# The modulation of the second block moved behind the projections of the first mixer, and four PSUM banks for projections

## The chip, the cores and the metric

The kernel runs on one core of one Trainium2 chip. The metric is the device time of one execution in microseconds (us). A measurement of this kernel is the median of several executions.

## The reference, cut to what matters

The reference is a transformer of two blocks on 256 tokens of width 1024, in float32. The first block is a hybrid mixer and a mixture of experts. The second is another mixer and another mixture, whose normed inputs are scaled and shifted by a modulation. The modulation depends on two small vectors alone and so can be computed at any time before the second block:

```
def modulation(cvec, w_ada, b_ada):          # w_ada: 1024 x 6144
    m = jax.nn.silu(cvec) @ w_ada + b_ada
    return jnp.split(m, 6, axis=-1)

def hybrid_mixer(n, w_in, gla_gate_w2, gla_gate_b, gla_norm_g, w_out):
    proj = n @ w_in                           # 1024 x 3088
    gq, gk, gv, gr, glr, aq, ak, av = jnp.split(proj, IN_SPLITS, axis=-1)
    log_a = jax.nn.log_sigmoid(glr @ gla_gate_w2 + gla_gate_b) / GLA_TAU
    o_gla = norm(gla_chunked(gq, gk, gv, log_a)) * jax.nn.silu(gr)
    o_att = three dilated softmax attentions of aq, ak, av
    return concatenate([o_gla, o_att]) @ w_out
```

## The kernel before

`mixer1` computes the first mixer and, between its steps, the modulation. Each engine has one list of instructions in a fixed order; semaphores tie the lists together.

**Weights.** All large weights come in pieces of 2 MB (1024 rows by 512 columns) into a ring of six slots, `weight_ring`. SyncE (SP) issues the loads one after the other, and for each it first waits until the slot's last reader is done. In `mixer1` these are the six pieces of `w_in` (0 to 5), the twelve pieces of `w_ada_2` for the modulation (ADA+0 to ADA+11), the two of `w_out` (WO, WO+1), and then four pieces of the first experts' weights for the phase that follows. `read_order` is the order in which the pieces are read, so that a load takes the slot that comes free first: w_ada pieces 0 to 5 are read between the projections, and their slots are free again for later pieces.

**Projections.** `project(j)` is one of 21 jobs on TensorE (PE). It multiplies the normed input `nT` by a part of a w_in piece (8 matmuls of 256 or 512 columns) into PSUM bank 4 + j % 2, and `take(j)` on ScalarE (ACT) copies the bank out. Job j waits until job j - 2 has been copied. `ps` has eight banks.

**The rest of PE's list.** `scores` and `p_transposes` belong to the attention, `weighted_values` is its last product. `level(l)` for l from 0 to 8 is a step of the gated linear attention. VectorE (DVE) makes its operand `M` (lines 708, 709) from `Dl` (line 684) after ACT has put `Dl` through an exponential (lines 523, 524), and copies the result out under a mask (line 694). The matmuls of line 443 give the output of the gated attention, DVE norms it, and `merge` (line 449) multiplies the result by `w_out` in two halves: the first (k from 4 to 7) needs the attention alone, the second the normed output.

**Modulation.** `mod_piece(i)` (line 390) multiplies 32 columns of `mcs` by w_ada piece i into bank 7, four matmuls side by side on column strips. `take_mod(i)` on ACT copies the bank out, and `mod_total(i)` (line 374) sums the strips into bank 6. PE's list has one such piece behind this or that projection or level: piece 0 behind project(10), 1 behind project(15), 2 behind the P transposes, 3 to 6 between levels and projections 17 to 20, 7 to 11 behind `weighted_values`. Projections 18 and 20 are cut in halves (`early`, `late`) around a level. After the modulation's last sum come line 443 and the merges.

```
            for half in range(2):
                pe.wait_ge(*has_come(WO + half))
            pe.wait_ge(s_pvtk, 2)
            merge(0, 0, range(4, 8))
```

PE waits here for both pieces of `w_out` before the first merge.

**After the mixer** `moe` begins behind a barrier of all engines: router, then a loop over the experts whose weights come through the same ring.

Of the kernel before, what the change touches and what calls it, by code (L numbers as in the profile page):

```python
# [12 lines left out]
P = 128  # L13
# [3 lines left out]
KD = D // P  # L17
# [111 lines left out]
def mixer1(c, t, mod):  # L129

    nc, ps, h = c.nc, c.ps, c.h
    with phase(nc, "m1_") as (st, sb, sem):
# [71 lines left out]
        w_cols = [1552, 2064, 0, 1024, 512, 2576]  # L204
        jobs = [("T", 0, i) for i in range(4)] + [("T", 1, i) for i in range(4)] + [("T", 2, i) for i in range(4)] + \
# [6 lines left out]
        ADA, WO, NX = 6, 6 + NP_, 8 + NP_  # L212
        read_order = [0, 1, ADA, 2, ADA + 1, 3, ADA + 2, ADA + 3, 4, ADA + 4, ADA + 5, 5] + [ADA + i for i in range(6, NP_)]
        label = {}
        slots = list(range(6))
        for x in range(6, NX):
            slots.append(slots[read_order[x - 6]])
        for s_, x in zip((3, 4, 0, 1, 2, 5), [WO, WO + 1] + read_order[NX - 6:]):
            label[slots[x]] = s_
        slots = [label[s_] for s_ in slots]  # L220
        nth = [slots[:x].count(slots[x]) + 1 for x in range(NX)]

        def has_come(x):
            return s_w[slots[x]], 16 * nth[x]

        def read(x):
            return (s_proj, done_with[x]) if x < 6 else (s_mpart, x - ADA + 1)
# [3 lines left out]
        @block.sync  # L231
        def _(sp):
            xv = t["x"].rearrange("b (t p) d -> p (b t) d", p=P)
            for tt in range(TT):
                sp.dma_start(h[:, tt, :], xv[:, tt, :]).then_inc(s_x[tt], 16)

            def load(x, w, a):
                if x >= 6:
                    sp.wait_ge(*read(read_order[x - 6]))
                sp.dma_start(piece(c, slots[x]), w[0, :, a:a + 512].rearrange("(k p) n -> p k n", p=P)).then_inc(s_w[slots[x]], 16)  # L240

            for x, a in enumerate(w_cols):
                load(x, t["w_in"], a)
            for i in range(NP_):
                load(ADA + i, t["w_ada_2"], i * BANK)
            for i in range(2):
                load(WO + i, t["w_out"], i * 512)
            W = [t[x] for x in ("expert_w1", "expert_w3", "expert_w2")]
            for x in read_order[NX - 6:]:
                sp.wait_ge(*read(x))  # L250
                load_one(c, sp, c.s_e1, slots[x] // 3, slots[x] % 3, W)
# [24 lines left out]
        @block.tensor  # L276
        def _(pe):
# [8 lines left out]
            def project(j, ks=range(KD)):  # L286
                kind, x, i = jobs[j]
                bank = 4 + j % 2
                if j >= 2 and ks[0] == 0:
                    pe.wait_ge(s_evac, j - 1)  # L290
                if kind in "TN" and i == 0:
                    pe.wait_ge(*has_come(x))
                w = piece(c, slots[x]) if kind in "TN" else None
# [3 lines left out]
                else:  # L297
                    if kind == "lr":
                        pe.wait_ge(s_lrw, 48)
                    for k in ks:  # L300
# [9 lines left out]
                if kind == "z" or ks[-1] == KD - 1:  # L310
                    last.then_inc(s_proj, 1)
# [21 lines left out]
            def weighted_values():  # L333
                pe.wait_ge(s_PTe, len(PT_GROUPS))
                pe.wait_ge(s_evac, NJ)
                for hh in range(4):
                    for it in range(TT):
                        for jt in range(it + 1):
                            for par in range(2):
# [3 lines left out]
                                last = pe.matmul(ps[par * 64:par * 64 + 64, 4 + hh // 2, at:at + P], av[:, jt, a * AHD:(a + 1) * AHD], p,  # L343
# [34 lines left out]
            def mod_piece(i):  # L378
                pe.wait_ge(*has_come(ADA + i))
                if i == 0:  # L380
                    pe.wait_ge(s_mcs, 1)
                    pe.wait_ge(s_pick, 1)
                    pe.wait_ge(s_mb, 16)
                    pe.matmul(ps[:, 6, 0:2 * NC], brow[:], each[:].rearrange("p k r -> p (k r)"), start=True, stop=False, skip_group_check=True)
                if i >= 1:
                    pe.wait_ge(s_mptk, i)
                w = piece(c, slots[ADA + i])
                for k in range(KD):
                    j = k % 4
                    last = pe.matmul(ps[32 * j:32 * j + 32, 7, :], mcs[:, k, :], w[:, k, :], start=(k < 4), stop=(k >= 4))  # L390
# [4 lines left out]
            early, late = range(0, 4), range(4, KD)  # L395
# [20 lines left out]
            project(18, early)  # L416
            level(1)
            project(18, late)
            mod_piece(4)
            level(2)  # L420
            project(19)
            level(3)
            mod_piece(5)
            project(20, early)
            level(4)
            project(20, late)
            mod_piece(6)
            level(5)
            weighted_values()
            mod_piece(7)  # L430
            level(6)
            mod_piece(8)
            mod_piece(9)
            level(7)
            mod_piece(10)
            mod_piece(11)
            level(8)
            mod_total(NP_ - 1)
            pe.wait_ge(s_Atk, NLV + 1)
            for i2 in range(TT):  # L440
# [4 lines left out]
                last.then_inc(s_og, 1)  # L445

            def merge(tt, half, ks):
                for k in ks:
                    last = pe.matmul(ps[:, 4 + 2 * half + tt, :], nT[:, k, tt * P:(tt + 1) * P], piece(c, slots[WO + half])[:, k, :],
# [23 lines left out]
        def _(act):  # L473
# [17 lines left out]
            def take(j):  # L491
                kind, x, i = jobs[j]
                bank = 4 + j % 2
# [19 lines left out]
            def take_mod(i):  # L513
# [3 lines left out]
                act.activation(mpart[:, i % 2, :], ps[:, 7, :], ACT.Copy).then_inc(s_mptk, 1)  # L517
# [8 lines left out]
            act.wait_ge(s_mc, 32)  # L526
            act.wait_ge(s_mz, 1)
            act.activation(mcs[:, :, 0:2], mc[:], ACT.Silu).then_inc(s_mcs, 1)
# [4 lines left out]
            take_mod(0)  # L533
            take(11)
            exps(1)
            for j in range(12, 16):
                take(j)
            take_mod(1)
# [9 lines left out]
            take_mod(2)  # L548
            take(17)
            level(1)  # L550
            take_mod(3)
            level(2)
            take(18)
            take_mod(4)
            level(3)
            take(19)
            level(4)
            take_mod(5)
            level(5)
            take(20)  # L560
            take_mod(6)
            level(6)
            for b in range(2):
                act.wait_ge(s_pv, b + 1)
                act.activation(catA[:, 2 * b:2 * b + 2, :].rearrange("p k n -> p (k n)"), ps[:, 4 + b, :], ACT.Copy).then_inc(s_pvtk, 1)
            take_mod(7)
            level(7)
            take_mod(8)
            take_mod(9)
            level(8)  # L570
            take_mod(10)
            take_mod(11)
# [1882 lines left out]
```

## Time and profile before

| | us |
|---|---|
| median of 3 runs | 1833.49 |
| lowest, highest | 1826.11, 1833.73 |
| the profiled execution: its own time | 1827.63 |
| the profiled execution: span from first to last instruction | 1825.5 |

Times within the span are counted from its first instruction. The profile tells for each engine when its instructions ran, what released them when they waited, what the DMA engines moved, and which clock TensorE was granted (1.00 is full speed, 0.50 the lower level). A line of the timeline has start, duration, engine, line of the code, operation, output and inputs, and the count of instructions merged into it. The records count two matmuls for each one of the code.

### The profile page before, as it was taken

How to read it: one execution, taken by the hardware profiler on the slowest of the kernel's cores; microseconds unless marked ns; L12 is line 12 of the kernel's file. 1: busy time of each engine (PE TensorE's matmuls, PEld its weight loads, DVE VectorE, ACT ScalarE, POOL GpSimd, SP SyncE). 2: the span in 40 equal slices, each digit the busy share in tenths (PEclk: the TensorE clock that was granted, in tenths of full speed). 3: DMA queues.
4: the chain of work that ended last, by engine and by line, in shares of the span. 5: the costliest groups of instructions: out<-in, count | busy, mean ns of one | idle time of the engine just before them, and what ended most of it. 6: DMA issues, size and time to landing. Idle time of an engine off the chain costs nothing. (4 is left out here: it accounts for less than half of the span.)

```text
span 1825.5 us, 29532 instructions
## 1 busy us (share of the span) xinstructions
PE 1465.0 (80%) x12551; PEld 975.3 (53%) x12551; DVE 628.8 (34%) x1703; ACT 258.1 (14%) x546; POOL 42.4 (2%) x61
## 2 busy tenths in 40 slices
PE   7999578999878887489998998989376666666664
PEld 6555345666555565279766746876243343333332
DVE  3533445222122332404765633432341222222224
ACT  2421221111011111021100212230010000000000
POOL 1000000000000000010000100000000000000000
PEclk9999689999888999789999999989688888888887
DMA  9677659999999999593231242244449999999994
GB/s 344 241 258 290 176 226 415 411 414 412 411 410 410 408 414 420 195 291 115 73 136 69 104 150 92 96 147 178 148 174 422 422 423 422 423 422 420 422 421 201
DMA packets 155736, 530.55 MB, mean 291 GB/s; under 512 B 38312, under 2 KB 56816, under 8 KB 139264
## 3 DMA queue, kind: packets, MB, share of 16 engines
q1 hardware_dynamic: 152016, 525.40, 73.1%
q0 software_dynamic: 1200, 3.77, 0.6%
q8 instruction: 68, 1.11, 0.2%
q10 hardware_dynamic: 2432, 0.10, 0.1%
q14 instruction: 20, 0.16, 0.0%
HBM read 528.19 MB, written 1.06 MB: 290 GB/s over the span
## 5 line engine op out<-in xcount | busy, mean ns | idle before, releaser
L1341 PE MATMUL ps<-weight_ring,e_xT 128*32 128x256 f32 x4096 | 310.1, 469 | 197.6 <-DMA weight_ring<-in_w_up_dram 134.7
L1341 PEld LDWEIGHTS ps<-weight_ring,e_xT 128*32 128x32 f32 x4096 | 173.8, 134 | 330.2 <-issue 284.2
L1363 PE MATMUL ps<-weight_ring,e_gT 128*32 128x256 f32 x2048 | 124.9, 385 | 17.7 <-DVE e_gT L1566 17.7
L1564 DVE TENSOR_TENSOR e_g<-e_act_g,ps 128x128 f32<-128x128 f32 x64 | 18.4, 287 | 300.2 <-ACT e_act_g L1407 299.1
L1363 PEld LDWEIGHTS ps<-weight_ring,e_gT 128*32 128x32 f32 x2048 | 60.3, 110 | 68.4 <-DVE e_gT L1566 28.8
L1563 DVE TENSOR_TENSOR e_act_g<-e_act_g,ps 128x128 f32<-128x128 f32 x32 | 9.2, 288 | 224.1 <-ACT e_act_g L1407 224.0
L1407 ACT ACTIVATE e_act_g<-ps 128x128 f32<-128x128 f32 x64 | 17.7, 277 | 478.1 <-PE ps L1341 478.1
L1318 PE MATMUL ps<-e_y,e_GwT 32*128 32x256 f32 x1056 | 75.6, 400 | 1.2 <-DVE e_GwT L1581 1.2
L961 PE MATMUL ps<-e_nT,e_ctx_w 128*128 128x256 f32 x320 | 72.3, 385 | 4.1 <-DVE e_ctx_gcols L1061 3.4
L1305 PE MATMUL ps<-e_n,e_Gt 128*32 128x256 f32 x1056 | 70.1, 381 | 0.0
L961 PEld LDWEIGHTS ps<-e_nT,e_ctx_w 128*128 128x128 f32 x320 | 61.0, 193 | 12.7 <-issue 3.6
L1566 DVE COPY e_gT<-ps 128x128 f32<-128x128 f32 x64 | 18.6, 291 | 133.9 <-PE ps L1311 133.9
L1318 PEld LDWEIGHTS ps<-e_y,e_GwT 32*128 32x128 f32 x1056 | 47.8, 184 | 29.8 <-issue 26.3
L1890 PEld LDWEIGHTS ps<-m_Q,weight_ring 128*128 128x128 f32 x480 | 56.2, 192 | 9.4 <-DVE m_Q L2191 5.7
L1890 PE MATMUL ps<-m_Q,weight_ring 128*128 128x128 f32 x480 | 57.3, 276 | 4.7 <-DVE m_Q L2191 4.7
L963 PE MATMUL ps<-e_ctx_w,e_nT 128*128 128x256 f32 x256 | 58.7, 382 | 0.5 <-DVE e_ctx_kw L1067 0.5
L1950 PE MATMUL ps<-weight_ring,m_nTp 128*128 128x512 f32 x128 | 58.4, 617 | 0.0
L1994 PE MATMUL ps<-m_nT,weight_ring 128*128 128x256 f32 x256 | 56.8, 382 | 0.0
L1855 PE MATMUL ps<-m_nT,weight_ring 128*128 128x256 f32 x256 | 56.4, 379 | 0.0
L1866 PE MATMUL ps<-weight_ring,m_nT 128*128 128x512 f32 x128 | 56.3, 592 | 0.0
L1994 PEld LDWEIGHTS ps<-m_nT,weight_ring 128*128 128x128 f32 x256 | 49.2, 192 | 6.9
L963 PEld LDWEIGHTS ps<-e_ctx_w,e_nT 128*128 128x128 f32 x256 | 47.4, 190 | 9.0 <-issue 2.3
(485 smaller groups left out, 1936.7 us busy)
## 6 DMA issues: line engine op xcount, KB each, us to landing
weight_ring<-in_expert_w_dram SPq DMA_DIRECT2D x96, 2048.0 KB, 20.4
weight_ring<-in_w_down_dram SPq DMA_DIRECT2D x32, 2048.0 KB, 24.6
weight_ring<-in_w_gate_dram SPq DMA_DIRECT2D x32, 2048.0 KB, 19.2
weight_ring<-in_w_up_dram SPq DMA_DIRECT2D x32, 2048.0 KB, 23.7
weight_ring<-in_w_in_dram SPq DMA_DIRECT2D x26, 2048.0 KB, 8.4
weight_ring<-in_w_ada_dram SPq DMA_DIRECT2D x12, 2048.0 KB, 7.9
e_ctx_w<-in_w_in_dram SPq DMA_DIRECT2D x18, 1024.0 KB, 22.2
weight_ring<-in_w_out_dram SPq DMA_DIRECT2D x4, 2048.0 KB, 10.3
```

The lines of the kernel that those rows point to most:

```text
L961: mm = pe.matmul(o, w[:, k, j * P:(j + 1) * P], nT[:, k, :], start=(k == 0), stop=(k == KD - 1))
L963: mm = pe.matmul(o, nT[:, k, j * P:(j + 1) * P], w[:, k, :], start=(k == 0), stop=False)
L1305: mm = pe.matmul(ps[32 * j:32 * j + 32, 5, 0:256], Gt[:, tt, :], n[:, tt, j * 256:(j + 1) * 256], start=(tt == 0), stop=(tt == TT - 1))
L1318: mm = pe.matmul(ps[:, m, tt * 256:(tt + 1) * 256], GwT[r, tt * P:(tt + 1) * P], y[r, :], start=False, stop=False, skip_group_check=True)
L1341: mm = pe.matmul(ps[32 * j:32 * j + 32, 4, 0:256].rearrange("p (w f) -> p w f", w=2), xT[:, k % 2, k // 2, :], w13[:, :, k, j * P:(j + 1) ...
L1363: mm = pe.matmul(ps[32 * m:32 * m + 32, 5, 0:256], gT[:, j * 32:(j + 1) * 32], w2[:, j, m * 256:(m + 1) * 256], start=(j == 0), stop=(j == ...
L1566: dve.tensor_copy(gT[:], ps[:, 4, 0:P]).then_inc(s_gT, 1)
L1855: mm = pe.matmul(ps[:, 4 + j % 4, 0:T], w[:, k, (j % 4) * P:(j % 4 + 1) * P], nT[:, k, :], start=(k == 0), stop=(k == KD - 1))
L1866: mm = pe.matmul(ps[:, 4 + j % 4, :], nT[:, k, tile * P:(tile + 1) * P], w[:, k, :], start=(k == 0), stop=(k == KD - 1))
L1890: mm = pe.matmul(o, a, b, start=True, stop=True)
L1950: mm = pe.matmul(ps[:, j % 4, :], nTp[:, k, tile * P:(tile + 1) * P], w[:, k, :], start=(k == 0), stop=(k == KD - 1))
L1994: mm = pe.matmul(ps[:, 2 + f % 2, 0:T], w[:, k, j * P:(j + 1) * P], rhs[:, k, :], start=(k == 0), stop=(k == KD - 1))
```

## The change

All twelve pieces of the modulation are moved behind `weighted_values` and level 4. The projections come first and use four banks (4 + j % 4), and job j waits for job j - 4. The modulation has banks 4 and 5 in turn for its products and 6 for its sums. `weighted_values` goes to banks 6 and 7. Pieces 0 and 1 stand before level 5, then two behind each of levels 5 and 6, two behind level 7, piece 8 behind level 8, and 9 to 11 behind the matmuls of line 443. Projections 18 and 20 are whole. The slots of the ring are taken in turn: w_ada piece i waits for the last projection that reads w_in piece i (i below 6), piece i from 6 on for `mod_piece(i - 6)`, the two pieces of w_out for `mod_piece(6)` and `mod_piece(7)`, the experts' four for pieces 8 to 11. Two small loads of `mod_c` by GpSimd (POOL) come later in its list, and the Silu that reads them moves behind take(12).

```diff
         w_cols = [1552, 2064, 0, 1024, 512, 2576]
+        RING = [3, 4, 0, 1, 2, 5]
...
             for x, a in enumerate(w_cols):
                 load(x, t["w_in"], a)
             for i in range(NP_):
-                load(ADA + i, t["w_ada_2"], i * BANK)
+                if i < 6:
+                    sp.wait_ge(s_proj, done_with[i])
+                else:
+                    sp.wait_ge(s_mpart, i - 5)
+                load(6 + i, t["w_ada_2"], i * BANK)
             for i in range(2):
+                sp.wait_ge(s_mpart, NP_ - 5 + i)
                 load(WO + i, t["w_out"], i * 512)
...
-            pool.dma_start(mc[:, :, 0], t["c_2"].rearrange("o (k p) -> p (o k)", p=P), allow_slow_non_contiguous=True).then_inc(s_mc, 16)
-            pool.dma_start(mc[:, :, 1], t["c_ctx_2"].rearrange("(k p) -> p k", p=P), allow_slow_non_contiguous=True).then_inc(s_mc, 16)
...
+            pool.dma_start(mc[:, :, 0], t["c_2"].rearrange("o (k p) -> p (o k)", p=P), allow_slow_non_contiguous=True).then_inc(s_mc, 16)
+            pool.dma_start(mc[:, :, 1], t["c_ctx_2"].rearrange("(k p) -> p k", p=P), allow_slow_non_contiguous=True).then_inc(s_mc, 16)
             pool.dma_start(brow[:], t["b_ada_2"].rearrange("o (k p) -> (o k) p", p=P)).then_inc(s_mb, 16)
...
-            def project(j, ks=range(KD)):
+            def project(j):
                 kind, x, i = jobs[j]
-                bank = 4 + j % 2
-                if j >= 2 and ks[0] == 0:
-                    pe.wait_ge(s_evac, j - 1)
+                bank = 4 + j % 4
+                if j >= 4:
+                    pe.wait_ge(s_evac, j - 3)
...
             def mod_piece(i):
-                pe.wait_ge(*has_come(ADA + i))
+                pe.wait_ge(*has_come(6 + i))
                 if i == 0:
...
+                    pe.wait_ge(s_pvtk, 2)
...
-                if i >= 1:
-                    pe.wait_ge(s_mptk, i)
+                if i >= 2:
+                    pe.wait_ge(s_mptk, i - 1)
...
-            project(10)
-            mod_piece(0)
-            for j in range(11, 16):
+            for j in range(10, 17):
                 project(j)
-            mod_piece(1)
-            project(16)
             for g in range(len(PT_GROUPS)):
                 p_transposes(g)
-            mod_piece(2)
             project(17)
             level(0)
+            project(18)
+            level(1)
+            project(19)
+            level(2)
+            project(20)
+            level(3)
+            weighted_values()
+            level(4)
+            mod_piece(0)
+            mod_piece(1)
+            level(5)
+            mod_piece(2)
             mod_piece(3)
...
             pe.wait_ge(s_Atk, NLV + 1)
...
                 last.then_inc(s_og, 1)
+            for i in range(9, NP_):
+                mod_piece(i)
+            mod_total(NP_ - 1)
...
             for half in range(2):
                 pe.wait_ge(*has_come(WO + half))
-            pe.wait_ge(s_pvtk, 2)
+            merge(1, 1, range(4, 8))
+            pe.wait_ge(s_mptk, NP_)
             merge(0, 0, range(4, 8))
             merge(1, 0, range(4, 8))
-            merge(1, 1, range(4, 8))
```

On ACT the copies follow the same order: levels 1 to 4 with takes 18 to 20, the two copies of the attention's output, then for each of levels 5 to 8 its exponentials and two `take_mod`, then the last four.

## Rows read from the trace of the kernel before

**Rows 1.** The first line of the page.

```profile
span 1825.5 us, 29532 instructions
```

**Rows 2.** Stretches: busy us of each engine (instructions), granted clock, DMA share, GB/s.

```profile
56.00:112.00 56.00, 55.94 (x286) 28.24 (x286) 22.13 (x25) 21.92 (x34) 0.00 (x0) 1.00 0.67 239
112.00:156.00 44.00, 44.00 (x350) 24.34 (x346) 15.67 (x31) 9.61 (x21) 0.00 (x0) 1.00 0.90 337
156.00:160.40 4.40, 4.40 (x26) 4.40 (x26) 2.09 (x4) 0.28 (x2) 0.00 (x0) 0.61 0.95 394
160.40:189.60 29.20, 28.96 (x76) 12.97 (x74) 8.36 (x13) 1.22 (x3) 1.67 (x1) 1.00 0.32 127
189.60:248.00 58.40, 36.39 (x236) 23.73 (x236) 25.84 (x91) 14.97 (x28) 3.22 (x10) 0.71 0.53 144
248.00:740.00 492.00, 418.65 (x4686) 277.60 (x4682) 148.12 (x489) 74.73 (x179) 0.00 (x0) 0.92 1.02 411
```

**Rows 3.** PE's waits from 0 to 200 us: total, times, longest.

```profile
PE ps L283 <- ACT m_n L483: 10.2, 1, 10.2
PE ps L305 <- DMA weight_ring<-in_w_in_dram: 0.8, 1, 0.8
```

**Rows 4.** Timeline of PE from 0 to 190 us.

```profile
120.33 1.92 PE L390 MATMUL ps<-weight_ring,m_mod_silu 128*32 128x512 f32 x16
122.18 1.05 PE L374 MATMUL ps<-m_mod_pick,m_mod_part 128*128 128x2 f32 x8
123.09 3.68 PE L307 MATMUL ps<-weight_ring,m_nT 128*128 128x512 f32 x8
126.70 1.16 PE L368 MATMUL ps<-m_M 64*128 64x128 f32 x16
...
131.43 1.92 PE L390 MATMUL ps<-weight_ring,m_mod_silu 128*32 128x512 f32 x16
...
135.36 0.66 PE L343 MATMUL ps<-m_PT,m_av 128*64 128x128 f32 x8
...
138.13 1.92 PE L390 MATMUL ps<-weight_ring,m_mod_silu 128*32 128x512 f32 x16
...
156.07 4.57 PE L443 MATMUL ps<-m_gv,m_AT 128*128 128x128 f32 x24
160.48 13.90 PE L449 MATMUL ps<-weight_ring,m_nT 128*128 128x512 f32 x32
...
175.50 14.00 PE L449 MATMUL ps<-weight_ring,m_nT 128*128 128x512 f32 x32
```

**Rows 5.** Timeline of DVE and ACT from 110 to 160 us.

```profile
120.44 1.36 DVE L694 COPY_PREDICATED m_AT<-mask_f,ps 128x512 f32<-128x512 uint8 x2 [5.58 <-PE ps L368]
...
122.63 0.42 DVE L709 TENSOR_TENSOR m_M<-m_Dl,m_qT 128x256 f32<-128x256 f32 x1
...
138.24 0.60 ACT L565 ACTIVATE m_nT<-ps 128x512 f32<-128x512 f32 x1 [0.71 <-PE ps L343]
```

**Rows 6.** Timeline of SP's queue from 0 to 250 us.

```profile
28.42 103.47 SPq L240 DMA_DIRECT2D weight_ring<-in_w_ada_dram  x12
133.41 7.07 SPq L240 DMA_DIRECT2D weight_ring<-in_w_out_dram  x2
```

**Rows 7.** Issues on the page (KB, median us to landing), and a stretch with the queue full.

```profile
weight_ring<-in_w_ada_dram SPq DMA_DIRECT2D x12, 2048.0 KB, 7.9
...
40.00:44.00 4.00, 4.00 (x21) 3.51 (x20) 0.00 (x0) 0.38 (x1) 0.00 (x0) 1.00 1.05 386
```

**Rows 8.** Two stretches of 1 us at the start.

```profile
7.00:8.00 1.00, 0.00 (x0) 0.00 (x0) 0.08 (x1) 0.89 (x2) 0.00 (x0) 1.00 1.58 141
...
12.00:13.00 1.00, 1.00 (x6) 1.00 (x5) 0.72 (x2) 0.25 (x1) 0.92 (x1) 1.00 1.10 372
```

**Rows 9.** Three stretches of 1 us behind the mixer.

```profile
194.00:195.00 1.00, 0.00 (x0) 0.00 (x0) 0.37 (x3) 0.00 (x0) 0.51 (x1) 0.50 0.87 133
...
204.00:205.00 1.00, 0.64 (x3) 0.64 (x4) 0.30 (x1) 0.65 (x2) 0.19 (x1) 0.50 1.05 348
...
207.00:208.00 1.00, 0.90 (x5) 0.63 (x3) 0.00 (x0) 0.66 (x2) 0.00 (x0) 0.68 1.15 492
```

More of the change, by code:

```diff
@@ L210, in mixer1, with slot_of @@
         done_with = [max(j + 1 for j, job in enumerate(jobs) if job[1] == x) for x in range(6)]
[L212 to L221, printed above, removed]
+        def slot_of(x):
+            return RING[x % 6]
         def has_come(x):
-            return s_w[slots[x]], 16 * nth[x]
-        def read(x):
-            return (s_proj, done_with[x]) if x < 6 else (s_mpart, x - ADA + 1)
+            return s_w[slot_of(x)], 16 * (x // 6) + 16
+        WO = 6 + NP_
         block = st.enter_context(nc.Block())
@@ L237, in load @@
             def load(x, w, a):
-                if x >= 6:
-                    sp.wait_ge(*read(read_order[x - 6]))
-                sp.dma_start(piece(c, slots[x]), w[0, :, a:a + 512].rearrange("(k p) n -> p k n", p=P)).then_inc(s_w[slots[x]], 16)
+                sp.dma_start(piece(c, slot_of(x)), w[0, :, a:a + 512].rearrange("(k p) n -> p k n", p=P)).then_inc(s_w[slot_of(x)], 16)
             for x, a in enumerate(w_cols):
@@ L244, in _ @@
             for i in range(NP_):
-                load(ADA + i, t["w_ada_2"], i * BANK)
+                if i < 6:
[3 more added lines that the diff above has]
+                load(6 + i, t["w_ada_2"], i * BANK)
             for i in range(2):
+                sp.wait_ge(s_mpart, NP_ - 5 + i)
                 load(WO + i, t["w_out"], i * 512)
             W = [t[x] for x in ("expert_w1", "expert_w3", "expert_w2")]
-            for x in read_order[NX - 6:]:
-                sp.wait_ge(*read(x))
-                load_one(c, sp, c.s_e1, slots[x] // 3, slots[x] % 3, W)
+            for i, (u, which) in enumerate(((0, 0), (0, 1), (0, 2), (1, 2))):
+                sp.wait_ge(s_mpart, NP_ - 3 + i)
+                load_one(c, sp, c.s_e1, u, which, W)
         @block.gpsimd
@@ L284, in _ @@
                 last.then_inc(s_tr, 1)
-            def project(j, ks=range(KD)):
+            def project(j):
                 kind, x, i = jobs[j]
-                bank = 4 + j % 2
-                if j >= 2 and ks[0] == 0:
-                    pe.wait_ge(s_evac, j - 1)
+                bank = 4 + j % 4
+                if j >= 4:
+                    pe.wait_ge(s_evac, j - 3)
                 if kind in "TN" and i == 0:
                     pe.wait_ge(*has_come(x))
-                w = piece(c, slots[x]) if kind in "TN" else None
+                w = piece(c, slot_of(x)) if kind in "TN" else None
                 if kind == "z":
@@ L299, in project @@
                         pe.wait_ge(s_lrw, 48)
-                    for k in ks:
+                    for k in range(KD):
                         if j == 0 and k % 2 == 0:
@@ L309, in project @@
                             last = pe.matmul(ps[0:GLR, bank, 0:T], w_lr[:, k, :], nT[:, k, :], start=first, stop=end)
-                if kind == "z" or ks[-1] == KD - 1:
-                    last.then_inc(s_proj, 1)
+                last.then_inc(s_proj, 1)
             def scores(it, heads, bank):
@@ L342, in weighted_values @@
                                 at = (hh % 2) * T + it * P
-                                last = pe.matmul(ps[par * 64:par * 64 + 64, 4 + hh // 2, at:at + P], av[:, jt, a * AHD:(a + 1) * AHD], p,
+                                last = pe.matmul(ps[par * 64:par * 64 + 64, 6 + hh // 2, at:at + P], av[:, jt, a * AHD:(a + 1) * AHD], p,
                                                  start=(jt == 0), stop=(jt == it))
@@ L383, in mod_piece @@
                     pe.wait_ge(s_mb, 16)
+                    pe.wait_ge(s_pvtk, 2)
                     pe.matmul(ps[:, 6, 0:2 * NC], brow[:], each[:].rearrange("p k r -> p (k r)"), start=True, stop=False, skip_group_check=True)
-                if i >= 1:
-                    pe.wait_ge(s_mptk, i)
-                w = piece(c, slots[ADA + i])
+                if i >= 2:
+                    pe.wait_ge(s_mptk, i - 1)
+                w = piece(c, slot_of(6 + i))
                 for k in range(KD):
                     j = k % 4
-                    last = pe.matmul(ps[32 * j:32 * j + 32, 7, :], mcs[:, k, :], w[:, k, :], start=(k < 4), stop=(k >= 4))
+                    last = pe.matmul(ps[32 * j:32 * j + 32, 4 + i % 2, :], mcs[:, k, :], w[:, k, :], start=(k < 4), stop=(k >= 4))
                 last.then_inc(s_mpart, 1)
@@ L393, in mod_piece @@
                     mod_total(i - 1)
-            early, late = range(0, 4), range(4, KD)
             for j in range(9):
@@ L403, in _ @@
             scores(1, range(4, 8), 0)
-            project(10)
-            mod_piece(0)
-            for j in range(11, 16):
+            for j in range(10, 17):
                 project(j)
-            mod_piece(1)
-            project(16)
             for g in range(len(PT_GROUPS)):
                 p_transposes(g)
-            mod_piece(2)
             project(17)
             level(0)
+            project(18)
[10 more added lines that the diff above has]
+            mod_piece(2)
             mod_piece(3)
-            project(18, early)
-            level(1)
-            project(18, late)
+            level(6)
             mod_piece(4)
-            level(2)
-            project(19)
-            level(3)
             mod_piece(5)
-            project(20, early)
-            level(4)
-            project(20, late)
+            level(7)
             mod_piece(6)
-            level(5)
-            weighted_values()
             mod_piece(7)
-            level(6)
+            level(8)
             mod_piece(8)
[L433 to L438, printed above, removed]
             pe.wait_ge(s_Atk, NLV + 1)
@@ L445, in _ @@
                 last.then_inc(s_og, 1)
+            for i in range(9, NP_):
+                mod_piece(i)
+            mod_total(NP_ - 1)
             def merge(tt, half, ks):
                 for k in ks:
-                    last = pe.matmul(ps[:, 4 + 2 * half + tt, :], nT[:, k, tt * P:(tt + 1) * P], piece(c, slots[WO + half])[:, k, :],
+                    last = pe.matmul(ps[:, 4 + 2 * half + tt, :], nT[:, k, tt * P:(tt + 1) * P], piece(c, slot_of(WO + half))[:, k, :],
                                      start=(k == 4), stop=(k == 3))
@@ L492, in take @@
                 kind, x, i = jobs[j]
-                bank = 4 + j % 2
+                bank = 4 + j % 4
                 act.wait_ge(s_proj, j + 1)
@@ L516, in take_mod @@
                     act.wait_ge(s_msum, i - 1)
-                act.activation(mpart[:, i % 2, :], ps[:, 7, :], ACT.Copy).then_inc(s_mptk, 1)
+                act.activation(mpart[:, i % 2, :], ps[:, 4 + i % 2, :], ACT.Copy).then_inc(s_mptk, 1)
             def level(l):
@@ L524, in level @@
                 act.activation(d[:, :, 1, :], d[:, :, 1, :], ACT.Exp, scale=1.0 / 16).then_inc(s_E, 1)
-            act.wait_ge(s_mc, 32)
-            act.wait_ge(s_mz, 1)
-            act.activation(mcs[:, :, 0:2], mc[:], ACT.Silu).then_inc(s_mcs, 1)
             for j in range(10):
@@ L532, in _ @@
             take(10)
-            take_mod(0)
             take(11)
             exps(1)
-            for j in range(12, 16):
+            take(12)
+            act.wait_ge(s_mc, 32)
+            act.wait_ge(s_mz, 1)
+            act.activation(mcs[:, :, 0:2], mc[:], ACT.Silu).then_inc(s_mcs, 1)
+            for j in range(13, 16):
                 take(j)
-            take_mod(1)
             act.wait_ge(s_az, 1)
@@ L547, in _ @@
                 act.activation(dst, ps[:, g % 4, :].rearrange("p (a n) -> p a n", a=4), ACT.Copy).then_inc(s_PTe, 1)
-            take_mod(2)
             take(17)
[L550 to L556, printed above, removed]
-            level(4)
[L558 to L562, printed above, removed]
+            for l in range(1, 4):
+                level(l)
+                take(17 + l)
+            level(4)
             for b in range(2):
                 act.wait_ge(s_pv, b + 1)
[L565 to L572, printed above, removed]
+                act.activation(catA[:, 2 * b:2 * b + 2, :].rearrange("p k n -> p (k n)"), ps[:, 6 + b, :], ACT.Copy).then_inc(s_pvtk, 1)
+            for l in range(5, NLV + 1):
+                level(l)
+                take_mod(2 * (l - 5))
+                take_mod(2 * (l - 5) + 1)
+            for i in range(8, NP_):
+                take_mod(i)
             act.wait_ge(s_msum, NP_)
```

## The prediction

> **What bounds the kernel now.** I read the stretches first. Of the 1825.5 us [rows 1], the first mixer takes the first 189.6. In it PE is busy in every microsecond from 56 to 189.6 at a granted clock of 1.00, but for 4.4 us at 0.61, while the DMA share is 0.67, 0.90 and 0.32 in the three long stretches [rows 2]. The list of PE's waits says the same: over 200 us PE waits twice, once before its first instruction and once 0.8 us for the first piece of w_in [rows 3]. So PE's own work sets the end of the mixer, and the DMA runs beside it with some idle time. Behind it come a serial router stretch at a DMA share of 0.53 and then the experts, with the DMA full at 411 GB/s for 492 us [rows 2]. The router stretch begins with the mixer's last result and the full DMA begins with the first experts' slots coming free, so a delay of the mixer should reach the end of the kernel whole.
>
> **Part 1, four banks instead of two.** The only thing this can remove is a wait of PE for a copy by ACT. No such wait is in the list [rows 3]. Worth: 0. The same goes for the modulation's two banks, and for projections 18 and 20 made whole.
>
> **Part 2, PE's order.** No matmul of the mixer is dropped or added, so PE's busy time stays. I follow its new list. A piece with its sum costs 123.09 - 120.33 = 2.76 us, a level 1.1, `weighted_values` 138.13 - 135.36 = 2.8 [rows 4]. Before, projection 20 ends at 131.43 [rows 4], and six pieces and levels 3 and 4 stood ahead of that which now stand behind it: 6 x 2.76 + 2 x 1.1 = 18.8. It ends at 112.6, or 111.6 with the gain of part 4. Level 3, weighted_values and level 4 take it to 116.6, where piece 0 begins.
>
> Three waits could open there. Level 4 needs its operand: from a level's start DVE needs its copy, the differences and two products, and is done 123.05 - 119.3 = 3.7 us later [rows 5], against 3.9 us of level 3 and weighted_values. Piece 0 now waits for ACT's copy of the attention's output, 0.1 + 0.6 us [rows 5], under level 4's 1.1. Levels 5 to 8 have two pieces, 5.5 us, over DVE's 3.7, and `take_mod` stands on ACT behind exponentials of a level whose differences come long before. I count all at 0. They are thin, though: without cover the first costs 3.7 - 1.1 = 2.6 us, and behind it on PE are all pieces and through them the loads.
>
> The block: 12 pieces 33.1, levels 5 to 8 about 4.0, line 443 4.4 as before, the last sum 0.5 more than the first piece saves: PE would be ready for the merges at about 158.6, against 160.48 [rows 4].
>
> **Part 3, the loads.** This is the part that counts. Before, w_ada's twelve issues spread from 28.4 to 131.9 and w_out's two came at 133.4 and 140.1 [rows 6], so both pieces of w_out were there before 160.48. Now pieces 0 to 5 sit in the slots that the projections free, and nothing frees a further slot until piece 0 is read. Its bias matmul and products take 2.2 us: 118.8. Only then can SP issue w_ada 6; 7 to 11 follow, then w_out 0 and 1. The issue of w_ada 6 lands 7.9 us later [rows 7], at 126.8. The seven pieces behind it come at the full rate: 2.097 MB at 386 GB/s [rows 7] is 5.43 us each, 38.0 in all. The issues are never later than that rate wants them: w_out 1 waits for piece 7, at about 142, and its data can only flow from 159. So w_out 1 lands at **164.8**, and PE has nothing to do from 158.6 to there: a new wait of 6.2 us. The modulation's own pieces are in time: 11 lands at 154, and is wanted at about 155.
>
> The first merge then begins at 164.8 instead of 160.48: +4.3 us. From there to the end it is 189.50 - 160.48 = 29.0 us as before [rows 4]. The normed output, which now has the time of pieces 9 to 11 for it, was hidden under the first merges and stays so, worth 0. The four experts' loads land by about 185, before the router begins, and the barrier waits for none of them.
>
> Bounds: the rate in the two stretches with w_out in flight is no lower than 337 GB/s as a mean with gaps [rows 2], 6.2 us a piece, which gives 170 (+9.7). From below, if w_ada 6's issue lands as a continuation of the stream (5.4 instead of 7.9), 162.3 (+1.8). I take 164.8, since the stream at 386 is the nearest row.
>
> **Part 4, the start.** The two small loads of mod_c go out at 1.8 and 2.9 us before and then stand in the DMA engines with x and the first piece of w_in. From 7 to 8 us the engines are busy (share 1.58) and move 141 GB/s, against 372 at 12 to 13 [rows 8]. PE's first projection waits for w_in [rows 3]. Behind the change these loads come after that. Lost bytes of this one stretch are 0.23 MB, 0.6 us; with its neighbours I take 1.0 us gained, between 0 (other small loads stay) and 1.3. The POOL queue's later entries, the bias rows and the zeroing of AT, keep their times within 1 us, and their readers come at 80 us or later. Silu behind take(12) is wanted at 116.
>
> **Part 5, the clock.** Behind the mixer PE is idle from 189.5, and by 194 the granted clock is at its lower level (0.50, 1.2 GHz) [rows 9]. After it begins again at 204.36 it has the lower one until about 207.6 [rows 9]: 3.3 us at half speed, 1.6 us lost. The new wait is 6.2 us, longer than the 4.5 after which the clock had fallen there, and sums with two columns come before it. So I add **1.6 us** to the merges; bounds 0 (no fall) and 3.2 (the same loss twice). The Trainium skill ("TensorE: Matmul & The Clock Gate", Part 1) says that the array runs at the lower clock after an idle stretch and gets the higher back by sustained work. The trace agrees, with 0.50 at 194 and again at the restart. By that rule alone the wait costs twice, once as a wait and once as slow merges; without it the sum would be 1.6 us less.
>
> **Sum.** +4.3 + 1.6 = **+5.9 us**, with the start's gain already in the 4.3. The span becomes 1831.4 and the profiled time 1827.63 + 5.9 = 1833.5. The median of the runs shown lies 5.9 above that profiled execution, so against it: 1839.4. The runs spread over 7.6 us; I say 1838.5.
>
> **Rivals.**
>
> *The block is slow (slower).* The granted clock was 0.61 from 156 to 160.4 [rows 2], right behind four pieces, sums and level 8 in a row, without any idle time; now there are twelve in a row. At the lower clock a piece costs up to twice 2.76. PE has 6.2 us to spare before w_out lands, so nothing happens up to about three pieces' worth at half speed; from there on each one is on the path. With half of the 42 us of the block at the lower clock, the merges begin at 180: +19 + 1, 1853. Against it: 112 to 156 held 1.00 with pieces, sums and levels in the same mix [rows 2]. By the rule of the Trainium skill cited above, a PE that is little used could lose its clock without a pause; the trace shows that once, at 156. It passes the 0.5% bound from some 9 us lost. Chance 0.13.
>
> *The loads are in time (no change or a trifle faster).* If w_out lands by 158.6, the end moves by 158.6 - 160.5 = -1.9: 1831.6. It would need eight pieces in 40 us from the first issue, 5.0 us each with no latency; rows 7 speak against it. Chance 0.07.
>
> *The delay is absorbed.* If the router or the experts waited for something that does not depend on the mixer, the +5.9 would be lost in it: 1833.5. The DMA moves almost nothing in the last of the mixer (0.32) and half in the router stretch [rows 2], so there is no backlog to wait for. Chance 0.08.
>
> My forecast has 0.72. Its own range is +2 to +9.7, 1831 to 1846 with the spread of the medians. For 8 in 10 with the rivals I give 1829 to 1850.
>
> A change of 0.5%, 9.2 us, is about what a measurement of this kernel can tell from none. The forecast lies within it but for its upper end (0.1 of it) and a lucky pair of medians; the slow block lies mostly beyond it; the other two are within. Slower by over 0.5%: 0.07 + 0.11 + 0.03 for what I do not see = 0.21; faster 0.04; same 0.75.
>
> **What the new profile would show.** Right: no wait of PE for ACT or DVE in the projections; projection 20 ends near 112; DMA idle or low between 60 and 112, then full from about 120 to 185; one wait of PE for `weight_ring<-in_w_out_dram` of about 6 us before line 449's first matmul, near 165; a clock of 0.50 just behind it; the mixer's last matmul at 195. Wrong: that wait under 3 us or over 10; waits of line 390 for w_ada pieces; a clock of 0.50 in several stretches between 117 and 159; first projection not earlier than 14.3. The number would be wrong without the steps being wrong if the granted clock of the later stages falls differently.

## The result and the profile after

The changed kernel has a median of 1840.68 us in 6 runs (1837.10 to 1843.60), against 1831.02 for the kernel before in 6 runs: a ratio of 1.0054, 95% interval 1.0036 to 1.0073. It is slower by 9.7 us. The forecast was 1838.5 in a range of 1829 to 1850, and the median lies in it. The ratio lies just over the bound of 0.5%, with that bound inside its interval, and to that side I had given 0.21.

The page of the changed kernel has these lines (the span, and the DMA's busy tenths in 40 slices of 46 us):

```profile
span 1836.4 us, 29529 instructions
...
DMA  9369559999999999583222242243439999999994
```

The page of the kernel before has in the place of the second line:

```profile
DMA  9677659999999999593231242244449999999994
```

The second slice has 3 tenths of DMA and had 6, since the old kernel had spread its loads over it. Of PE's waits up to 200 us (total, times, longest), two are new against [rows 3], and the 0.8 us for the first piece of w_in are gone:

```profile
PE ps L278 <- ACT m_n L472: 10.3, 1, 10.3
PE ps L438 <- DMA weight_ring<-in_w_out_dram: 7.2, 1, 7.2
PE ps L385 <- DMA weight_ring<-in_w_ada_dram: 1.3, 1, 1.3
```

The timeline of PE answers to [rows 4] (lines 362, 385, 368, 429 and 438 are 368, 390, 374, 443 and 449 before):

```profile
13.69 31.25 PE L300 MATMUL ps<-m_nT,weight_ring 128*128 128x256 f32 x144
...
111.34 1.16 PE L362 MATMUL ps<-m_M 64*128 64x128 f32 x16
...
116.20 0.36 PE L379 MATMUL ps<-m_mod_each,m_mod_bias_rows 48*128 48x96 f32 x2
...
144.76 2.92 PE L429 MATMUL ps<-m_gv,m_AT 128*128 128x128 f32 x24
...
154.65 1.92 PE L385 MATMUL ps<-weight_ring,m_mod_silu 128*32 128x512 f32 x16 [1.29 <-DMA weight_ring<-in_w_ada_dram]
156.50 1.95 PE L368 MATMUL ps<-m_mod_pick,m_mod_part 128*128 128x2 f32 x16
165.64 16.44 PE L438 MATMUL ps<-weight_ring,m_nT 128*128 128x512 f32 x32 [7.19 <-DMA weight_ring<-in_w_out_dram]
181.92 1.04 PE L453 MATMUL ps<-ident,m_n 128*128 128x128 f32 x8
...
183.20 14.00 PE L438 MATMUL ps<-weight_ring,m_nT 128*128 128x512 f32 x32
```

PE is done with the modulation at 158.45 and begins the first merge at 165.64. The first merges take 181.92 - 165.64 = 16.28 us against 174.21 - 160.48 = 13.73 before, where this line follows the merges of [rows 4]:

```profile
174.21 1.04 PE L464 MATMUL ps<-ident,m_n 128*128 128x128 f32 x8
```

The mixer's last matmul ends at 197.20 instead of 189.50. Stretches (busy time of each engine, granted clock, DMA share, GB/s) show both halves of the loss:

```profile
80.00:112.00 32.00, 32.00 (x123) 15.21 (x123) 7.73 (x15) 6.67 (x15) 0.00 (x0) 1.00 0.34 122
112.00:120.00 8.00, 8.00 (x108) 5.04 (x104) 5.19 (x10) 3.06 (x8) 0.00 (x0) 1.00 0.83 271
120.00:156.00 36.00, 34.71 (x324) 19.97 (x320) 15.89 (x29) 7.80 (x16) 1.68 (x1) 1.00 1.04 384
...
158.00:160.00 2.00, 0.45 (x4) 0.36 (x4) 0.00 (x0) 0.29 (x2) 0.00 (x0) 1.00 1.05 385
160.00:162.00 2.00, 0.00 (x0) 0.00 (x0) 0.00 (x0) 0.00 (x0) 0.00 (x0) 0.59 1.06 390
...
168.00:170.00 2.00, 2.00 (x3) 0.67 (x2) 0.00 (x0) 0.00 (x0) 0.00 (x0) 0.50 1.00 426
170.00:172.00 2.00, 2.00 (x5) 0.91 (x4) 0.00 (x0) 0.00 (x0) 0.00 (x0) 0.85 1.00 426
172.00:174.00 2.00, 2.00 (x6) 0.95 (x5) 0.00 (x0) 0.00 (x0) 0.00 (x0) 1.00 0.91 381
```

SP's queue agrees, by the time of each issue and its time to landing. w_ada 6 is issued at 118.5, when piece 0 has been read, and lands at 126.4. The two pieces of w_out land at 160.1 and 165.5. In the kernel before they had landed at 145.8 and 151.2, 9 us ahead of the first merge. From 80 to 112 the DMA is a third busy, and from 120 to 156 it is full; it stays so until the experts' pieces are in, at 184. The idle time of the one is the wait of the other. In the pause the granted clock falls to its lower level, and the merges run their first 5 us there.

### The profile page after: what moved, and what is told of

Its sections match the earlier page's. It is cut to its first block and busy times, and to the rows that moved or that the text cites. A ratio compares the mean times of both kernels' runs of the same rounds, so it can differ in the third digit from the quotient of the medians.

```text
span 1836.4 us, 29529 instructions
## 1 busy us (share of the span) xinstructions
PE 1465.1 (80%) x12551; PEld 975.7 (53%) x12551; DVE 629.3 (34%) x1703; ACT 255.7 (14%) x544; POOL 42.5 (2%) x61
```

## The experiments

There are ten runs, in three groups, each group on one chip with the kernel before beside it. The ratios compare within a group. A difference between two medians of different groups is less sure than that. The table at the end of the section has all runs. Line numbers shift a little from run to run.

**Leave six loads out.** The edit in the changed kernel; the waits' counts follow it:

```diff
                     sp.wait_ge(s_mpart, i - 5)
-                load(6 + i, t["w_ada_2"], i * BANK)
+                if i < 6:
+                    load(6 + i, t["w_ada_2"], i * BANK)
```

> The changed kernel without the loads of w_ada pieces 6 to 11: these six pieces multiply what pieces 0 to 5 left in their slots, so the modulation's second half is computed from the wrong weights and PE's work is the same. Theory (w_out lands late because twelve MB of w_ada stand ahead of it): w_out is asked for at 143.9 and there by 152, so PE has no wait; the pieces end at 157.2, the first merge starts there at the full clock, the mixer's last matmul ends at 186 to 187 instead of 197.2, time 10.5 to 11.5 us under the changed kernel and some 3 under the one before. Rival (the block of pieces itself, or its order, is what costs): the wait goes, but the mixer still ends later than 189.5 and the time stays above the kernel before.

PE's timeline of that run:

```profile
154.99 1.95 PE L374 MATMUL ps<-m_mod_pick,m_mod_part 128*128 128x2 f32 x16
156.80 13.98 PE L444 MATMUL ps<-weight_ring,m_nT 128*128 128x512 f32 x32
170.62 1.04 PE L459 MATMUL ps<-ident,m_n 128*128 128x128 f32 x8
...
171.90 14.00 PE L444 MATMUL ps<-weight_ring,m_nT 128*128 128x512 f32 x32
```

PE has no wait, the clock stays at 1.00, and the mixer ends at 185.90. The time is 1829.81 us, 10.9 below the changed kernel and 1.0 below the kernel before in its group, which is within the interval; some 3 had been expected. PE's list in the new order is not dearer than the old one; the loads are the whole cost. The list is even a little shorter: from the first projection to the first merge it takes 156.80 - 13.55 = 143.25 us, against 159.06 - 14.51 = 144.55 in the second profile of the kernel before, further down. The forecast had only 0.6 us for that; the rest was not followed up.

**Leave one load out.** As above with `if i < 11`.

> The changed kernel without the load of w_ada piece 11 alone, which uses piece 5's weights again: one load of 2 MB less in the queue ahead of w_out. Theory (every 2 MB ahead of w_out is 5.4 us of the merge's start): w_out lands at 160.2, PE waits 3.0 instead of 7.2 us, and if so short a pause leaves the granted clock at 1.00 the merges take 13.7 instead of 16.3; the mixer ends at 189.3 (191 if the clock falls), time 6 to 8 us under the changed kernel. Rival (w_out waits for its slot, not for the queue): w_out lands where it did, within 1 us, and the time stays.

The wait for w_out was 3.1 us, as worked out:

```profile
161.44 16.40 PE L444 MATMUL ps<-weight_ring,m_nT 128*128 128x512 f32 x32 [3.10 <-DMA weight_ring<-in_w_out_dram]
```

But the clock fell all the same. Stretches of that run:

```profile
158.00:159.00 1.00, 0.35 (x4) 0.26 (x3) 0.00 (x0) 0.28 (x2) 0.00 (x0) 1.00 1.05 385
159.00:160.00 1.00, 0.00 (x0) 0.00 (x0) 0.00 (x0) 0.00 (x0) 0.00 (x0) 0.76 1.25 500
160.00:161.00 1.00, 0.00 (x0) 0.00 (x0) 0.00 (x0) 0.00 (x0) 0.00 (x0) 0.50 1.08 449
```

The merges took 16.2 us; the mixer ended at 192.97, where 191 had been expected for a clock that falls. In this execution PE's projections also ran 1.2 us longer at the start, so that the merges began 4.2 us earlier and not 5.4. The time is 1835.47, 5.2 lower, and less than the expected 6 to 8. The rival, that w_out waited for its slot, is out.

**Fill the pause.** In the changed kernel:

```diff
+            for _ in range(8):
+                pe.matmul(ps[:, 3, :], c.ident[:], cnt[:].rearrange("p t n -> p (t n)"), start=True, stop=True)
             for half in range(2):
                 pe.wait_ge(*has_come(WO + half))
```

> The changed kernel with eight more matmuls of 128x512 into the idle bank 3, of operands that lie there anyway, ahead of the wait for w_out (some 6.9 us of the 7.2 us wait). Theory (the wait costs twice, as a pause and by the clock at its lower level behind it): the granted clock stays at 1.00 through the merges, the first sixteen merges' matmuls take 13.7 us instead of 16.3, the mixer ends 2.5 us earlier at 194.7 and the time is 2.5 us lower. Rival (the clock falls by the modulation's pieces, not by the pause): the clock is 0.50 in some stretch behind 157 all the same and nothing is gained; 0 to +1 us.

The timeline of PE:

```profile
158.55 7.11 PE L443 MATMUL ps<-m_cnt,ident 128*128 128x512 f32 x16
165.96 13.97 PE L438 MATMUL ps<-weight_ring,m_nT 128*128 128x512 f32 x32 [0.30 <-DMA weight_ring<-in_w_out_dram]
179.76 1.04 PE L455 MATMUL ps<-ident,m_n 128*128 128x128 f32 x8
```

The transposes of the normed output begin at 179.76, so the first merges took 13.8 us. The mixer ended at 195.05 instead of 197.20. The clock's part of the loss is shown in the profile: 2.5 us in the merges. The time, 1838.95, is 1.7 lower, which the intervals can't tell from none.

**Two banks again.** The changed kernel with `bank = 4 + j % 2` and the wait of before for job j - 2.

> The changed kernel with the projections on two banks in turn instead of four, as before the change. Theory (PE never waited for a bank): projection 20 ends at the same 111.3, the mixer at 197.2, time within 1 us of the changed kernel. Rival (the four banks took up some of ACT's delays and hid part of the loss): waits of PE for ACT appear at the projections and the time is 1 to 3 us higher.

No wait of PE for ACT appears. From the first projection to the first piece of the modulation it took 116.25 - 13.13 = 103.1 us against 116.49 - 13.69 = 102.8 with four banks; the mixer ended at 196.75. The time is the median of 4 runs, 1838.10, within the spread. Four banks buy nothing that can be measured.

**Wait for each half of w_out by itself.** In the changed kernel:

```diff
-            for half in range(2):
-                pe.wait_ge(*has_come(WO + half))
-            merge(1, 1, range(4, 8))
             pe.wait_ge(s_mptk, NP_)
+            pe.wait_ge(*has_come(WO))
             merge(0, 0, range(4, 8))
             merge(1, 0, range(4, 8))
+            pe.wait_ge(*has_come(WO + 1))
+            merge(1, 1, range(4, 8))
```

> The changed kernel in which the first merges wait for what they read only: the two merges of the first half of w_out wait for w_out 0, and merge(1, 1) behind them for w_out 1. Theory (the merges wait for the loads' queue, 5.4 us a piece): w_out 0 lands at 160.2 and w_out 1 at 165.6, under the 6.9 us of the first two merges; PE waits 1.8 us instead of 7.2 and the mixer ends 5.4 us earlier at 191.8 (189.4 if the granted clock stays up in so short a pause), time 5 to 8 us under the changed kernel. Rival (what is late is not w_out): no gain, within 1 us.

```profile
PE ps L438 <- DMA weight_ring<-in_w_out_dram: 2.3, 1, 2.3
```

The row is from PE's waits. The mixer ended at 191.33, 5.9 us earlier. The time is 1833.31; above the kernel before of its group that is 3.5 us, where the changed kernel lay 9.7 above, so about 6 us are gained (7.5 by the ratios). The clock fell in this pause of 2.3 us too: it was 0.50 from 161 to 163, and the first merges took 15.3 us.

**Three pieces early, nine in the block.** Built on the kernel before. `mod_piece(0)`, `(1)` and `(2)` keep their old places and bank 7, projections use banks 4 and 5, the two late loads of mod_c are taken over, and:

```diff
-        read_order = [0, 1, ADA, 2, ADA + 1, 3, ADA + 2, ADA + 3, 4, ADA + 4, ADA + 5, 5] + [ADA + i for i in range(6, NP_)]
+        read_order = [0, 1, ADA, 2, ADA + 1, 3, ADA + 2, 4, 5] + [ADA + i for i in range(3, NP_)]
...
             level(3)
             weighted_values()
             level(4)
+            mod_piece(3)
+            mod_piece(4)
             level(5)
...
                 last.then_inc(s_og, 1)
+            mod_piece(11)
+            mod_total(NP_ - 1)
```

> The changed kernel's list with two banks for the projections and pieces 0, 1 and 2 of the modulation put back behind project(10), project(15) and the P transposes on bank 7, their slots given to w_ada pieces 3 and 5 and 8, and nine pieces in the block, two of them between level 8 and the first merge but for line 443. Theory (only the time at which the first pieces free their slots matters): w_out 1 lands near 150, PE has no wait, the mixer ends at 186 to 187, as in the run without six loads, with all the work done: 10 to 12 us under the changed kernel and 1 to 3 us under the one before. Rival (pieces between projections cost PE something that the block saves): the projections' stretch is over 8.3 us longer (three pieces), and the mixer ends no earlier than 189.5.

PE had no wait after its first instruction, and its last piece stands directly before the merges:

```profile
152.38 2.92 PE L443 MATMUL ps<-m_gv,m_AT 128*128 128x128 f32 x24
155.23 1.92 PE L394 MATMUL ps<-weight_ring,m_mod_silu 128*32 128x512 f32 x16
157.09 1.95 PE L374 MATMUL ps<-m_mod_pick,m_mod_part 128*128 128x2 f32 x16
158.90 13.98 PE L451 MATMUL ps<-weight_ring,m_nT 128*128 128x512 f32 x32
```

The mixer ended at 188.00, against an expected 186 to 187. The first 144 matmuls of the projections took 32.31 us here and 31.25 in the changed kernel's first profile. The time is 1828.64, 12 us below the changed kernel, and 11 if each is taken against the kernel before of its own group. Against the kernel before the ratio is 0.9991 (0.9980 to 1.0002), so a gain over it is not shown. Three slots freed early were enough to bring w_out in time, but only just. By SP's queue w_out 1 was issued at 141.3 and landed at 158.4, half a microsecond before the first merge, where I had expected it near 150.

**The small loads alone.** The kernel before with the two loads of mod_c moved in POOL's list as in the change.

> The kernel before with one part of the change alone: the two small loads of mod_c later in POOL's list, and the Silu that reads them behind take(7). Theory (they slow the first piece of w_in): the stretch from 7 to 8 us moves over 350 GB/s instead of 141, the first projection begins at 13.1 to 13.8 instead of 14.31, the mixer ends 0.5 to 1 us earlier, and the time is 0.5 to 1 us lower, less than can be told from none. Rival (the start is bound by x and its norm): first projection at 14.3.

The stretch from 7 to 8 us moved 355 GB/s, and the first projection began at 13.77 instead of 14.31. The dip came later instead, with the two loads: from 15 to 17 us it was 160 and 179 GB/s. And line 443, in the old order, took 2.94 us:

```profile
155.64 2.94 PE L443 MATMUL ps<-m_gv,m_AT 128*128 128x128 f32 x24
158.42 13.90 PE L449 MATMUL ps<-weight_ring,m_nT 128*128 128x512 f32 x32
```

The mixer ended at 187.44. Of the 2.1 us against 189.50, 0.4 came from the start (line 443 began at 155.64 instead of 156.07) and 1.6 from the clock, which had not fallen. The time is 1827.89, a ratio of 0.9991 (0.9977 to 1.0006), which can't be told from none.

**Line 443 ahead of the last piece.** The kernel before, with level 8 and line 443 ahead of `mod_piece(11)` and its sums.

> The kernel before with level 8 and the matmuls of line 443 ahead of the modulation's last piece instead of behind it. Theory (the granted clock fell at 156 because pieces, two sums in a row and level 8 came together just there): line 443 takes 2.9 us as in the changed kernel instead of 4.57, and the mixer ends 1.6 us earlier at 187.9. Rival (the clock falls somewhere anyway): the 0.50 stretch shows in the merges instead and the mixer ends at 189.5 or later.

Line 443 took 2.94 us behind a wait of 0.9 us for DVE; the mixer ended at 188.86. Since the run with the small loads showed the same 2.94 in the old order, this says nothing of the order. The test was inconclusive. The time is 1831.41, the ratio 0.9998 (0.9984 to 1.0013).

**A second profile of both kernels**, unchanged.

> The kernel before, unchanged, for a second look at its profile. Theory (the fall of the granted clock at 156 in its first profile was chance, since the same order of instructions half a microsecond earlier showed none): line 443 takes 2.9 or 4.6 us as it falls out, the mixer ends between 187.9 and 189.6, and the stretch from the mixer's last matmul to the end of the span differs from the first look's 1636.0 by some microseconds in either direction. Rival (the order of pieces, sums and level 8 brings the fall about): 4.57 us again and 189.5 again. The time is that of the kernel before within 0.2%.

> The changed kernel, unchanged, for a second look at its profile and its time. Theory (the mixer's 7.7 us are the whole loss, and the other 3.2 us between the two profiled spans are the scatter of the later stages): the wait for w_out is 7.0 to 7.3 us again, the mixer ends at 197, but what follows it to the end of the span is 1632 to 1642 us instead of 1639.2, and the time against the kernel before is 1.004 to 1.005. Rival (the change costs the later stages some 2 to 3 us as well): 1639 or more again and a ratio of 1.0055 or more.

The kernel before, its timeline of PE:

```profile
156.27 2.94 PE L443 MATMUL ps<-m_gv,m_AT 128*128 128x128 f32 x24
159.06 13.90 PE L449 MATMUL ps<-weight_ring,m_nT 128*128 128x512 f32 x32
...
174.08 14.00 PE L449 MATMUL ps<-weight_ring,m_nT 128*128 128x512 f32 x32
```

The changed kernel:

```profile
155.62 1.92 PE L385 MATMUL ps<-weight_ring,m_mod_silu 128*32 128x512 f32 x16 [1.39 <-DMA weight_ring<-in_w_ada_dram]
157.48 1.95 PE L368 MATMUL ps<-m_mod_pick,m_mod_part 128*128 128x2 f32 x16
166.66 16.78 PE L438 MATMUL ps<-weight_ring,m_nT 128*128 128x512 f32 x32 [7.23 <-DMA weight_ring<-in_w_out_dram]
...
184.56 14.00 PE L438 MATMUL ps<-weight_ring,m_nT 128*128 128x512 f32 x32
```

The fall of the clock at 156 in the first profile of before was chance: the same kernel ran without it here. Without it that mixer ends at 188.08. The changed one ended at 198.56, where 197 had been expected. Its ratio in this group is 1.0060 (1.0042 to 1.0078). From the last matmul of the mixer to the end of the span it took 1838.0 - 198.56 = 1639.4 us. So both signs of the rival, a ratio of 1.0055 or more and a rest of 1639 or more, came true, and the theory's 1.004 to 1.005 did not. The rival's cause, a cost in the later stages, does not follow from them. The kernel before had 1826.4 - 188.08 = 1638.3 for the rest, only 1.1 less, and the table shows rests of other variants of the changed kernel from 1632.5 to 1641.8. The larger ratio comes from the mixer: the loss in it is 198.56 - 188.08 = 10.5 us, not 7.7.

All runs, with the time at which the mixer's last matmul ends in the profiled execution and what followed it there:

| run | mixer ends | rest of the span | median | ratio to before (95%) |
|---|---|---|---|---|
| before, first profile | 189.50 | 1636.0 | 1831.02 | |
| before, second profile | 188.08 | 1638.3 | 1831.30 | 0.9999 (0.9989 to 1.0010) |
| changed | 197.20 | 1639.2 | 1840.68 | 1.0054 (1.0036 to 1.0073) |
| changed, second profile | 198.56 | 1639.4 | 1840.48 | 1.0060 (1.0042 to 1.0078) |
| six loads out | 185.90 | 1636.7 | 1829.81 | 0.9995 (0.9983 to 1.0007) |
| one load out | 192.97 | 1632.5 | 1835.47 | 1.0029 (1.0019 to 1.0039) |
| pause filled | 195.05 | 1641.8 | 1838.95 | 1.0045 (1.0028 to 1.0062) |
| two banks | 196.75 | 1635.5 | 1838.10 | 1.0044 (1.0027 to 1.0061) |
| split wait | 191.33 | 1638.1 | 1833.31 | 1.0013 (1.0001 to 1.0025) |
| three early | 188.00 | 1640.4 | 1828.64 | 0.9991 (0.9980 to 1.0002) |
| small loads late | 187.44 | 1635.5 | 1827.89 | 0.9991 (0.9977 to 1.0006) |
| line 443 first | 188.86 | 1644.4 | 1831.41 | 0.9998 (0.9984 to 1.0013) |

The rest of the span scatters over 12 us and does not follow the kernel. The median less the mixer's end lies between 1640.5 and 1643.9 in all twelve rows, while the mixer's end itself moves by 12.7: what the mixer loses, the kernel loses, to within 3 us.

## Why the prediction was right, and where it was off

**The step that decided was right.** Pieces in the old order free slots early and let w_ada 6 onward and w_out flow under the projections. In the block nothing frees a seventh slot before piece 0 is read, and eight pieces of 2 MB then stand between that moment and the merges. I had worked out that the first merge could begin at 164.8; it began at 165.64. The issue and landing of w_ada 6 came 0.4 us earlier than forecast (126.4 for 126.8), and the seven pieces behind it took 39.1 us for 38.0. Leaving out six loads, one load, or half of the wait, and freeing three slots early, moved the mixer's end to within 2 us of what the queue's arithmetic says.

**PE's list.** Projection 20 was to end at 111.6 and ended at 111.3, piece 0 to begin at 116.6 and began at 116.2. The three thin covers held, with no wait of PE for DVE or ACT. One thing failed, and it was on my list of signs of being wrong: PE waited for a piece of w_ada. I had w_ada 11 land at 154 and be wanted at 155. It was wanted at 153.4, since line 443 took 2.92 us and not the 4.4 that I had taken over from before, and PE waited 1.3 us for it. That cost nothing, as w_out was later still. But it makes the nearly exact readiness for the merges, 158.45 for 158.6, partly luck: 1.5 us too much for line 443 and a wait of 1.3 us left out cancel.

**The clock** was mis-sized. I had 1.6 us from one restart behind the mixer; the merges lost 16.28 - 13.73 = 2.55 in the first profile and 16.62 - 13.73 = 2.9 in the second. The pause is followed by about 5 us at the lower level, not 3.3. The price varies between executions: by the same subtraction it was 1.6 us in the run that waits for each half by itself and 2.5 with one load out. The Trainium skill ("TensorE: Matmul & The Clock Gate", Part 1) says that the array runs at the lower clock after an idle stretch. By that rule a pause is paid twice, and the trace agrees: filling it gave the merges back 2.5 us.

**The start** gained 0.6 us against the first profile of before where I had 1.0. The slow stretch did not vanish, it moved: in the changed kernel 15 to 16 us moves 175 GB/s, behind the first piece of w_in.

**The base of the sum was off by 1.4 us.** This is the largest of three reasons that the forecast of +5.9 came out low, beside 0.8 us of w_out and 1.0 us of the clock. Together they are the 3.2 us between 5.9 and 197.20 - 188.08 = 9.1. I made the sum against a mixer that ended at 189.50, with line 443 at a granted clock of 0.61, and carried its 4.4 us into the new order. That fall was chance: it was there in one of three profiles of the old order of that stretch. Against 188.08 the two profiles of the changed kernel are 9.1 and 10.5 us later, and the medians say 9.7 and 9.5. Terms: w_out late, 165.64 - 159.06 = 6.6 (166.66: 7.6); clock 2.55 (2.9).

**The rivals.** The slow block is out: the granted clock was 1.00 from 112 to 160. (Its sum had a slip: 6.2 us to spare are 2.2 pieces at half speed, not three.) Loads in time is out by the 7.2 us wait. An absorbed delay is out by the table, in which the medians follow the mixer's end. The four banks are worth nothing, as forecast.

**The range** held, and part of that is luck. The median of the kernel before was taken as 1833.49 from three runs and is 1831.02 from six; that error of +2.5 us made up for part of a change that was forecast too small. On the true base +5.9 gives 1836.9, 3.8 below the measured 1840.68. The chance of 0.75 for a change within 0.5% was too high. The upper bound of +9.7 was that of w_out's landing alone: with the clock's 0 to 3.2 us it is +12.9, well past the bound of 9.2, and that end deserved more than a tenth.

## What to carry to other kernels

A ring of slots turns the order of reads into the order of loads: work that is moved behind other work takes its slot releases with it, and whoever loads next through the ring pays. Before moving a block of weight-reading work, count the bytes that must pass between the block's first release and the next consumer behind it, at the measured rate, and compare that with the block's own time. Releasing three slots early was enough here, with 0.5 us to spare, and waiting for each piece by itself instead of for both gave back 5.9 us of the mixer with four lines. And take a second profile of the kernel before: a fall of the clock that happens in one execution of three should not become the base of a sum.

## What was not expected of the hardware

The granted clock fell after shorter pauses than the 4.5 us seen behind the mixer. Behind the block of pieces and two-column sums, pauses of 2.3, 3.1, 7.1, 7.2 and 7.2 us all ended at the lower level. With one load out, PE's last matmul ended at 158.35 and the clock was 0.50 from 160 on. With no pause there, or one of under 1 us, it fell in one execution of seven (at 156 in the first profile of before, PE busy throughout). What decides this is not shown; no run varied the work ahead of a pause of the same length.

In three executions (one load out, three early, the changed kernel's second profile) the first 144 matmuls of the projections took 32.0 to 32.4 us instead of 31.25, at a granted clock of 1.00, with the loss between 14 and 16 us. The cause stays open; no run was made for it.
